# Four sequence mixers in one hand-ordered stage: one common order of steps against one order per engine, and a masked product and sum against a predicated copy

## What the reference computes

```python
a = rms_norm(h, ln_mix_pre); proj = a @ w_in            # split into the inputs of four mixers
y_a = s5_mixer(...)      # scan, then y = gelu(y); y = y * sigmoid(y @ w_glu); rms_norm over 256 channels
y_b = hgrn2_mixer(...)   # gated linear attention, chunks of 64, 4 heads of 64: decays exp(b_t - b_s)
y_c = fox_mixer(...)     # softmax attention with forget gates; then a norm per head
y_d = mlstm_mixer(...)   # q, k = silu(conv(q, k)); weights exp(...), h = num / max(|den|, exp(-m))
# y_b and y_d end in headwise_rms_norm(o) times silu(g) and sigmoid(o); y_c in headwise_rms_norm
mix = concat([y_a, y_b, y_c, y_d]) @ w_out
```

## Time and profile before

| | |
|---|---|
| median of three executions | 2335.56 us |
| the profiled execution | 2339.18 us, its span 2337.4 us |
| busy in the span | PE 92%, DVE 53%, ACT 35%, POOL 12% |
| mean granted TensorE clock | 0.958 |
| the stage of this case | 1743.25 to 1890.1 us of the span, 146.85 us |
| busy in the stage | PE 91.1, DVE 67.1, ACT 51.4, POOL 10.2 us; mean granted clock 0.72 |

### The profile page before, as it was taken

How to read it: one execution, slowest core, us unless ns; L and a number is a source line. 1 busy time by engine, 2 the same in 40 slices (tenths; PEclk the granted TensorE clock), 3 DMA queues, 4 the chain that set the end, 5 groups by cost and what they waited for, 6 DMA issues and landing times. The chain is left out here.

```text
span 2337.4 us, 30101 instructions
## 1 busy us (share of the span) xinstructions
PE 2159.2 (92%) x12276; PEld 1713.2 (73%) x12276; DVE 1247.4 (53%) x1688; ACT 821.1 (35%) x1295; POOL 271.0 (12%) x273
## 2 busy tenths in 40 slices
PE   8899988999999989999899999999995679999996
PEld 6777876778878778887687888775663457878875
DVE  5547756642443566665643443575584445633544
ACT  3344223531332434444532233352233244322321
POOL 0000002000001000000205910204441000000002
PEclk9999998999999999999999999999997779999998
DMA  5110002222222122221132222231100021323221
GB/s 216 64 64 28 3 3 86 85 90 99 99 82 100 64 81 73 73 72 46 63 113 90 96 98 95 90 112 56 49 23 1 1 108 66 113 74 118 92 77 66
DMA packets 50601, 177.08 MB, mean 76 GB/s; under 512 B 5616, under 2 KB 5616, under 8 KB 50208
## 3 DMA queue, kind: packets, MB, share of 16 engines
q1 hardware_dynamic: 46800, 163.86, 20.4%
q10 hardware_dynamic: 3168, 7.60, 0.9%
q0 software_dynamic: 496, 3.69, 0.4%
HBM read 170.94 MB, written 4.19 MB: 75 GB/s over the span
## 5 line engine op out<-in xcount | busy, mean ns | idle before, releaser
L1104 DVE TENSOR_TENSOR w_lo<-w_raw,w_hi 128x1024 fp32r<-128x1024 f32 (+1 forms) x320 | 411.2, 1286 | 756.1 <-ACT w_hi L1097 756.0
L1202 PE MATMUL banks<-xh,w_hi 128*128 128x512 f32 x1560 | 628.0, 403 | 3.6 <-PEq L213 3.6
L1204 PE MATMUL banks<-xh,w_lo 128*128 128x512 f32 x1560 | 612.6, 393 | 0.0
L1203 PE MATMUL banks<-xl,w_hi 128*128 128x512 f32 x1560 | 612.0, 392 | 0.0
L1097 ACT ACTIVATE w_hi<-w_raw 128x1024 fp32r<-128x1024 f32 (+1 forms) x320 | 328.6, 1029 | 732.6 <-PE banks L1204 690.7
L1202 PEld LDWEIGHTS banks<-xh,w_hi 128*128 128x128 f32 x1560 | 295.9, 190 | 87.5 <-issue 21.9
L1204 PEld LDWEIGHTS banks<-xh,w_lo 128*128 128x128 f32 x1560 | 295.1, 189 | 63.7
L1203 PEld LDWEIGHTS banks<-xl,w_hi 128*128 128x128 f32 x1560 | 296.0, 190 | 59.2 <-issue 1.7
L1202 PE MATMUL banks<-hh,w_hi 128*128 128x512 f32 x688 | 272.0, 395 | 11.7 <-DVE w_lo L1104 4.8
L1203 PE MATMUL banks<-hl,w_hi 128*128 128x512 f32 x688 | 269.4, 392 | 0.0
L1204 PE MATMUL banks<-hh,w_lo 128*128 128x512 f32 x688 | 269.1, 391 | 0.0
(11 more groups left out here) (507 smaller groups left out, 2713.2 us busy)
## 6 DMA issues: line engine op xcount, KB each, us to landing
w_raw<-in_w SPq DMA_DIRECT2D x128, 512.0 KB, 3.2
w_raw<-in_w_gu SPq DMA_DIRECT2D x44, 512.0 KB, 3.2
w_raw<-in_w_c_in SPq DMA_DIRECT2D x40, 512.0 KB, 3.2
w_raw<-in_w_ab_in SPq DMA_DIRECT2D x27, 512.0 KB, 3.3
w_raw<-in_w_in SPq DMA_DIRECT2D x25, 512.0 KB, 3.2
w_raw<-in_w_down SPq DMA_DIRECT2D x16, 384.0 KB, 3.0
w_raw<-in_w_down SPq DMA_DIRECT2D x16, 320.0 KB, 2.8
w_raw<-in_w_ab_out SPq DMA_DIRECT2D x8, 512.0 KB, 3.3
```

The lines of the kernel that those rows point to most:

```text
L1104: dve.tensor_tensor(lo[:, 0:n], core.raw[u % RAW][:, 0:n], hi[:, 0:n].bitcast(F32), ALU.subtract).then_inc(core.split_ready, 1)
L1202: pe.matmul(bank, hi[:, w], src.xh[:, kk, :], start=kk == 0, stop=False)
L1203: pe.matmul(bank, hi[:, w], src.xl[:, kk, :], start=False, stop=False)
L1204: mm = pe.matmul(bank, lo[:, w], src.xh[:, kk, :], start=False, stop=last)
```

## The change

All of it lies in `late_mixers` and its four classes. The common list goes; the steps are cut into finer methods and each of ACT, DVE and PE has its own written-out list. The other edits:

- `gather`: for all but the diagonal (i = 0), product and sum become one predicated copy from the banks into S where the mask is set. The tile `part` goes.
- ACT loads the table set "sigmoid_and_others" at the start and does the two Tanh and all Sigmoids before it loads the log and exp set.
- the mlstm bound goes through bank 2, ahead of the items, and both halves have tiles of their own (`low[0]`, `low[1]`).
- the norms have two tiles of squares and two of inverses; the gate times gain is multiplied into Y before the inverse is there (`gate`), and silu(g) of tiles 2 and 3 is made ahead; their order is 4, 5, 6, 2, 3, 7.

```diff
     def gather(self, dve, i):
...
-        to = (self.part if i else self.S)[:].rearrange("p c n t -> p (c n) t")
+        to = self.S[:].rearrange("p c n t -> p (c n) t")
         dve.wait_ge(s.pairs, i + 1)
-        if i > 1:
-            dve.wait_ge(s.summed, i - 1)
-        dve.tensor_tensor(to, bank, mask, ALU.mult).then_inc(s.masked, 1)
-        if i:
-            dve.wait_ge(s.masked, i + 1)
-            dve.tensor_tensor(self.S[:], self.S[:], self.part[:], ALU.add).then_inc(s.summed, 1)
+        if i == 0:
+            dve.tensor_tensor(to, bank, mask.broadcast_to([P, 2 * NCH, C]), ALU.mult).then_inc(s.masked, 1)
+        else:
+            dve.wait_ge(s.masked, i)
+            dve.copy_predicated(to, mask.bitcast(mybir.dt.uint32).broadcast_to([P, 2 * NCH, C]), bank).then_inc(s.masked, 1)
...
+    def bound(self, pe, c):
+        if c:
+            pe.wait_ge(s.low_out, c)
+        for e in range(2):
+            mm = pe.matmul(core.psum[2][HALF_ROWS[e], :], sel[ml, 2 * c + e, 0:64], self.low_row, start=True, stop=True)
+        mm.then_inc(s.lows, 1)
...
+    def gate(self, dve, k):
+        dve.wait_ge(s.squared, self.ORDER.index(k) + 1)
+        dve.wait_ge(s.sig, list(self.GATES).index(k) + 1)
+        if k in (2, 3):
+            dve.wait_ge(s.silu, k - 1)
+        dve.scalar_tensor_tensor(y, y, self.core.param("gain", k), self.sig[k][:], ALU.mult, ALU.mult).then_inc(s.gated, 1)
...
-        order = [(scan, 0), (scan, 1), (mlstm, "begin"), (hgrn, "keys"), (mlstm, "sig"), (scan, 2), (mlstm, "silu"), (norms, "sig"),
-                 (scan, 3), (hgrn, "carry"), (scan, 4), (hgrn, 0), (mlstm, 0), (norms, 4), (mlstm, 1), (hgrn, 1), (mlstm, 2), (norms, 5),
-                 (mlstm, 3), (hgrn, 2), (mlstm, 4), (mlstm, 5), (hgrn, 3), (mlstm, 6), (mlstm, 7), (hgrn, 4), (mlstm, 8),
-                 (mlstm, 9), (hgrn, 5), (mlstm, 10), (hgrn, "last"), (mlstm, 11), (hgrn, "states"), (mlstm, 12), (hgrn, "out"),
-                 (mlstm, 13), (norms, 2), (mlstm, 14), (norms, 3), (mlstm, 15), (norms, 6), (norms, 7)]
```

More of the change, by code:

```diff
@@ L1936, in score @@
         pe.matmul(core.psum[5][:, 0:P], core.mask("identb"), core.mask("prev"), start=False, stop=True).then_inc(s.scores, 1)
[L1938 to L1977, removed]
@@ new lines, in _ @@
+            norms.square(act, 4)
+            hgrn.keys_out(act, 0)
+            norms.square(act, 5)
+            mlstm.weight(act, 4)
+            hgrn.span(act, 3)
+            mlstm.sums(act, 0)
+            hgrn.keys_out(act, 1)
+            mlstm.weight(act, 5)
+            hgrn.span(act, 4)
+            norms.inverse(act, 4)
+            mlstm.weight(act, 6)
+            hgrn.span(act, 5)
+            mlstm.weight(act, 7)
+            mlstm.sums(act, 1)
+            mlstm.weight(act, 8)
@@ new lines, in _ @@
+            mlstm.invert(act, 0)
+            mlstm.weight(act, 9)
+            norms.inverse(act, 5)
+            mlstm.weight(act, 10)
+            norms.square(act, 6)
+            mlstm.weight(act, 11)
+            mlstm.weight(act, 12)
+            mlstm.sums(act, 2)
+            mlstm.weight(act, 13)
+            norms.inverse(act, 6)
+            hgrn.out(act, 0)
+            mlstm.weight(act, 14)
+            norms.square(act, 2)
+            hgrn.out(act, 1)
+            mlstm.weight(act, 15)
@@ L2682, in _ @@
+            norms.square(act, 3)
+            norms.inverse(act, 2)
+            mlstm.sums(act, 3)
+            mlstm.invert(act, 1)
+            norms.inverse(act, 3)
+            norms.square(act, 7)
+            norms.inverse(act, 7)
         @block.vector
         def _(dve):
-            for part, step in order:
-                part.dve(dve, step)
+            scan.cubic(dve)
+            hgrn.to_end(dve)
+            scan.gelu(dve, 0)
+            scan.gelu(dve, 1)
+            mlstm.split(dve)
@@ new lines, in _ @@
+            mlstm.bound(pe, 0)
+            scan.gate(pe, 0)
+            scan.gate(pe, 1)
+            hgrn.diagonal(pe)
+            mlstm.score(pe, 0)
+            mlstm.score(pe, 1)
+            scan.total(pe)
+            pe.wait_ge(scan.s.inv, 1)
+            mlstm.heads(pe, 0)
+            mlstm.score(pe, 2)
+            mlstm.bound(pe, 1)
+            hgrn.spans(pe, 0)
+            mlstm.heads(pe, 1)
+            mlstm.score(pe, 3)
+            mlstm.heads(pe, 2)
+            pe.wait_ge(mlstm.s.low_out, 2)
```

705 lines of the change are left out of this document (426 added, 279 removed).

## The result

Four executions of the changed kernel have a median of 2278.86 us (2274.24 to 2279.19); four of the kernel before, the later one among them, have 2335.01. The ratio is 0.9752, with a 95% interval from 0.973 to 0.9773. The forecast of 2278 (2270 to 2293) holds. The profiled execution took 2279.19 us, its span 2277.4.

The account below looks back on a forecast made before the run. One stage of 146.85 us, bound by turns between engines, adds whole to the time. Stretches of 29.3 + 24.8 + 7.2 + 6.2 + 19.9 sum to 87.4 us, 89 taken, 57.9 less: 2278 us, range 2270 to 2293.

Parts of the forecast that it names:

- The bound: Stage of late_mixers, 146.85 us, added whole to the kernel's time; bound by turns taken, no engine full.
- the chain named: Between spans, the common list puts DVE's gather behind a norm needing PE's newest work; DVE waited 7.42 us.
- the second stretch: First to sixth span's pairs on PE: 64.5 us before, 24.8 laid out, 39.7 less, PE and DVE level.
- The last three stretches: Sixth span's pairs to products, to outputs, to stage's end: 7.2, 6.2 and 19.9 us; 6.65, 5.7 and 35.5 before.
- The copy: Predicated copy on DVE in each gather but the diagonal's: taken at 1.22 us, bounds 0.6 to 2.36; six sums go.
- POOL beside DVE: First to sixth span's pairs: DVE's products of two SBUF tiles held by POOL four times for 1.5 to 2 us.
- The one pass of sigmoids: Up to the first span's pairs: saves a table load on ACT, which isn't last there; gain nothing.
- The step that failed: Assumption for the whole stage: PE runs at the lower clock behind its longest waits, 5.6 us of it laid out.
- the layout: New lists laid out instruction by instruction: stage 87.4 us summed, 89 taken; same method gave 148.6 for the old lists.
- the first stretch: Stage's start to the first span's pairs: 34.5 us before, 29.3 laid out, 5.2 less.
- the clock stays down: Rival: PE's clock stays low in the new order; half its work at 1.2 GHz gives stage 113, time 2302; 7%.
- The layout's other checks: Signs in the stage: first to sixth pairs 25 us, no new wait over 2 before pairs 1 to 5, few long DVE waits.

Follow-up runs that it names:

- old_order_copy: The kernel before with the predicated copy alone, in place of masked product and sum; ratio 0.9973, stage 139.5 us.
- new_order_sum: The changed kernel with masked product and sum in place of the predicated copy; 2282.51 us, ratio 0.9777, stage 91.3 us.
- silu_first: The changed kernel with DVE's four SiLUs put ahead of gather 0; ratio 0.9754, stage 90.8 us.
- copy_twice: The changed kernel with each of the six predicated copies made twice, same result; ratio 0.9774, stage 93.1 us.
- fill_gap: silu_first plus 68 unread 64x64 instructions on PE behind score 0, while it would wait for weight 0; ratio 0.9719, stage 82.7 us.
- weight0_first: silu_first plus, on ACT, mlstm's weight 0 ahead of the bound and S5's two squares; ratio 0.9711, 2271 us, stage 85.4 us.

## Why the prediction was right, and where it wasn't

**The bound, and where the time came from: right.** The stage's gain went whole to the kernel (behind the stage both spans have 447 us), and the chain named (a gather behind a norm that depends on PE's newest work) was what the lists removed: the second stretch fell from 64.5 to 26.7 us, with no wait for a norm ahead of a gather.

**The last three stretches: right to 0.1 us,** 7.2, 6.2 and 19.9. The chain behind the last outputs is the one laid out, its last block sum at the lower clock:

```profile
1826.05 2.04 PE L2687 MATMUL banks<-late_norm_sq,consts 128*128 128x512 f32 x2 [4.46 <-ACT late_norm_sq L2666]
```

**The copy: right.** 1.30 us for 1.22, nearest to the row that it was taken from; the 1.19 estimated from the Trainium skill ("VectorE: DVE Perf Modes", The TRN2 errata) is 0.11 off. The six rows are one group of the source view:

```profile
L2178 DVE COPY_PREDICATED late_hg_S<-consts,banks x6: 1292/1298/1308, 1774.0 to 1800.4; 128x1024 f32<-128x1024 uint32 x6
```

Its removal of the six sums was priced at 7.3 us or more, and old_order_copy shows 7.4. In the new order the sums would only have cost 3.8, as new_order_sum shows. (The ratio of old_order_copy, 0.9973, is 6.3 us.)

**POOL beside DVE: the hold right, the count high.** The first product of W took 2.29 us (above), and ended 0.55 us behind POOL's instruction, so it was held for about as long as that ran; 0.69 is what 512 columns take alone. Between the first and the sixth span's pairs that happened twice and not four times, and once more from just ahead of them. POOL's instruction beside the product shown:

```profile
1782.84 1.93 POOL L2093 TENSOR_TENSOR hg_delta<-hg_b 128x1024 f32<-128x1024 f32 x1 [3.22 <-ACT late_hg_W L2123]
```

**The one pass of sigmoids: costed at nothing, and not shown apart.** No run isolates it. What is seen is that the load that stays is in the way as soon as the SiLUs are early (silu_first).

**The step that failed** is "PE is taken at the lower clock behind its longest waits, as it ran behind those of 6.29 and 3.78 us": the level is right, but how long it lasts was taken too short. In the layout the clock is back in time for part of the S5 sum (2.4 us for two tiles) and for all behind it. The trace has 3.73 for that sum, and 5.5 us from the first head sum to the pairs (1764.75 to 1770.24) against 2.7. That is 1.3 + 2.8 = 4.1 us, the whole of the first stretch's miss of 3.8; the first span's pairs at 3.68 for 2.1 are most of the second's 1.9. In new_order_sum and copy_twice, with the same code and the same wait, the S5 sum has 3.01 us, the head sum 1.13, and the stretch its forecast 29.3 but for 0.3. So the term is one that differs between executions, and the forecast gave it one value. Why the clock came back early in two profiled executions and late in the third stays open. fill_gap shows that it is the clock and not the turns between the engines: with it held, the first two stretches are 49.6 us, below the layout's 54.1, since the SiLUs are early there as well.

**Two terms that cancel.** Score 0 began 17.8 us into the stage, and the layout has the SiLUs done at 17.5, but not by right terms: w_glu was to begin at 7.7 and take 4.0 us, and it began at 6.6 (DVE was done with the cubic 1.3 us sooner than the 5.3 us laid out) and took 5.3 to the diagonal.

**The rival "the clock stays down"** held for one stretch, 20.4 us, out of the 93. Its sign, a window in mid-stage granted 0.50, is there, and the mean clock is 0.82 where 0.95 was expected; the 86% of PE's busy time (over 75% was named) is partly work at half speed. Its evidence was in the earlier trace rows: 8.61 of 10 us busy at 0.50. The forecast gave it 7% as a rule for half or all of PE's work, and otherwise only room in the range, where it should have been a term. Its price doesn't follow from the terms beside it either: half of 67 us at half the clock is 33.5 us more, 27.9 above the 5.6 of the layout and not some 24, and all of it 61.4, not 55.5; no row shows what would hide the rest.

The Trainium skill's "TensorE: Matmul & The Clock Gate" (A second HAM failure mode) was cited for this rival. Its case is a clock that goes up and down between groups. Here it fell behind a wait of 3.73 us (2.83 in silu_first) and stayed low for 17 to 20 us; once it was up, waits of up to 0.70 us left it at 1.00 from 1775.6 to 1823.2, with PE busy for 44.99 of 47.60 us (1.6 us of the rest are the start of its 4.46 us wait near the end).

**The layout's other checks.** First to sixth pairs: 26.7 (25 said). No wait before pairs 1 to 5 over 0.70 (2 said). DVE's waits over 3 us: 4.55 for the diagonal and 5.11 at the outputs, both named.

## What to carry to other kernels

Where several engines share one list, look for a step that sits behind another part's step which depends on the newest work of a third engine: here that order, with the clock that its waits had cost, was nine tenths of the gain, and the finer pieces in the old order gave none beyond the copy. Lay such a list out engine by engine with the durations of the trace, and cost each wait of PE twice: as the wait, and as the work behind it at half clock. In these runs even waits of 1.3 to 1.4 us had work at the lower clock behind them (w_glu 6.54 for 5.40 us, the S5 sum 3.53 for 1.93), and the low stretch behind one of 3.73 us differed in cost by 3.5 us between executions; give such a term a range. A list written by hand is worth laying out a second time once it runs; two moves took 7.75 us more off the stage, and 8 off the median.

## What was not expected of the hardware

- A PE that is nearly full doesn't have its clock back: 18.85 of 20.40 us busy, at 0.50 throughout, and the last 10.6 us of it without a gap. It is not the kind of product either: 64 dense 64x64 products ran at 0.50 there (3.68 us), and in new_order_sum the clock came back in the middle of fp32 products of 512 columns (the S5 sum, 3.01 us) behind the same wait.
- Unread products can hold the clock: 2.20 us of them in a wait took about 7 us off the stage. Making the wait shorter by order (weight0_first) did nearly the same.
- Code that was not changed took 6.2 us more in one execution than in another ahead of the stage, and the same first stretch took 33.1 us in one and 29.6 in two others. So a single profile tells a difference of a few us only where the granted clocks are alike.
